# Building the state space's matrices on VectorE, in four parts between turns of an FFN's loop, instead of on GpSimd

## Chip, cores and metric

One core of one Trainium2 chip. The metric is the time of one execution of the whole program on the device, in microseconds; the median of three runs before the change is 1818.07 us (1816.41 to 1823.21).

## What is computed

A stack of four layers (256 tokens, width 1024) and one block of a second model behind it. Each layer is a mixer (attention, spatial gating, S5 state space, attention) and a gated FFN with a causal convolution of three taps. This case touches the preparation of the third layer's state space, cut here to what it computes:

```python
def s5_layer(xn, w_in, lam_re, lam_im, log_dt, b_re, b_im, c_re, c_im, d_skip, w_glu):
    ...
    mag = jnp.exp(dt * lr)
    ar = mag * jnp.cos(dt * li)
    ai = mag * jnp.sin(dt * li)
    den = lr * lr + li * li
    coef_re = ((ar - 1.0) * lr + ai * li) / den
    coef_im = (ai * lr - (ar - 1.0) * li) / den
    bbar_re = coef_re[..., None] * br32 - coef_im[..., None] * bi32
    bbar_im = coef_re[..., None] * bi32 + coef_im[..., None] * br32
    bu_re = jnp.einsum('gph,blgh->blgp', bbar_re, ug)
    ...

def conv_gated_ffn(xn, w_up, conv_w, conv_b, w_down):
    h = causal_depthwise_conv(xn @ w_up, conv_w, conv_b)
    a, g = jnp.split(h, 2, axis=-1)
    return (jax.nn.silu(g) * a) @ w_down
```

The kernel also needs the products of the decay (ar, ai) with c_re and c_im, since it works on two time steps at once.

## The kernel before

The program is written out by hand for five engines, which meet only at semaphores. SyncE streams the weights from memory in units of 128 x 2048 fp32 into a ring of three (`raw`). ScalarE rounds each unit to `whi` (`split_hi`, L385), VectorE makes the rest `wlo = raw - whi` (`split_lo`, L911), and TensorE multiplies each pair of tiles three times (L1752 to L1754: high by high, high by low, low by high). So TensorE cannot begin a unit before its L911 has ended.

An FFN has 33 units: 22 "up" and 11 "down". Two up units stand ahead of a loop of nine turns, written as a hardware loop on each engine; a turn is two up units and one down unit, and a last group of the same form follows. In a turn VectorE does, for each of the two up units: the scaling of the result out of PSUM (L1122, waits for TensorE), a split (L911, waits for ScalarE), the four convolution taps (L1136, two SBUF inputs each), a product with the gate (L1143, waits for ScalarE's SiLU at L500); then the third split and the low part of the hidden tile (L1156). The order on each engine is the order of the code, so whatever stands in front of an L911 delays it. Behind the last unit VectorE adds the result to the stream (L1200) and makes the next layer's low operand (L955). `split_hi` and `split_lo` run up to three units ahead of TensorE.

`ffn(layer, aside=None, then=None)` takes a function `aside`. With one, the loop is cut by `parts(n, cut)` into pieces of two turns, and `aside(p)` is called ahead of piece p:

```python
    return [(i, min(i + 2, n)) for i in range(0, n, 2)] if cut else [(0, n)]
...
                for p, (b, e) in enumerate(parts(n - 1, aside)):
                    if aside:
                        aside(p)
                    with dve.Fori(0, e - b) as it:
```

The nine turns make five pieces. Before the change only the fourth FFN has such a function, on ScalarE (`context_high`) and on VectorE (`context_operand`, L1087 to L1093).

GpSimd has little to do: `square_sums` (L2504) for each norm, `discretize` between the fourth and the fifth of them, during the second FFN, and later `first_inputs`, `shifted_outputs` and some products in the state space. `discretize` makes, in one chain in which almost every instruction waits for the one before it (`link`): exp(dt lr) by a polynomial on 128 x 32 (L2407 to L2418), MG as its square spread over 64 columns (L2419, L2420), a cleared area and CRE and CIM out of the DMA'd matrices SBC (L2423 to L2429), the decay ARE and AIM (L2431, L2432), the two-step decay and its 64th power (L2433 to L2443), the coefficients CFR and CFI (L2445 to L2453), and then the matrices: XB[0] from CFR, CFI and B, C2D from ARE, AIM and C (L2456 to L2469, on 64 or 128 partitions by 512). The last one sets `s5_set`, for which TensorE waits in `turn(0)` (L2276), after the first unit of the state space.

## Time and profile before

| | us |
|---|---|
| median of three runs (lowest, highest) | 1818.07 (1816.41, 1823.21) |
| the profiled execution, by the clock of the runs | 1819.32 |
| its span, first to last instruction | 1817.5 |
| TensorE (PE) busy | 1710.2, 94% |
| VectorE (DVE) busy | 1246.4, 69% |
| ScalarE (ACT) busy | 841.6, 46% |
| GpSimd (POOL) busy | 158.1, 9% |
| mean granted TensorE clock | 0.974 of full speed |

The page's chain of work that ended last is 65% TensorE and 17% VectorE. Times of instructions are counted from the start of the span. A wait in square brackets stands ahead of the instruction, with the one that ended it behind the arrow. Where an engine is busy all the time, a faster neighbour changes nothing; a change pays where it shortens a wait of the engine that sets the pace.

### The profile page before, as it was taken

Reading aid. Unit: us, or ns where it says so; the run is one execution under the profiler, and the core shown is the slowest. Engines: PE = TensorE matmul, PEld = TensorE weight load, DVE = VectorE, ACT = ScalarE, POOL = GpSimd, SP = SyncE. Lnnn points to the kernel's source line nnn. Section 1 sums busy time; section 2 is a strip of 40 time slices with the busy share of each in tenths; the row PEclk is TensorE's granted clock in tenths of the full one; section 3 lists DMA queues with packets and bytes.
Section 4 is the critical chain, followed back from the end, with each engine's and each line's share of the span. In section 5 each row is a group of like instructions: output and inputs, shape, how many; then the busy total and the mean of one; then the engine's idle time right before and its main releaser. Section 6 shows DMA issues by size and latency. Waiting matters only on the chain.

```text
span 1817.5 us, 34773 instructions
## 1 busy us (share of the span) xinstructions
PE 1710.2 (94%) x14525; PEld 1617.6 (89%) x14525; DVE 1246.4 (69%) x1592; ACT 841.6 (46%) x958; POOL 158.1 (9%) x128
## 2 busy tenths in 40 slices
PE   6999999999899998899999999999989999999997
PEld 6979999899899985699999988999988479889997
DVE  5847777786877759857777774777775575654444
ACT  5355555546445530255455445555555533143343
POOL 1002000104910062100000100100000000000000
PEclk9999999899999998999999999999989999899999
DMA  7804555535445522454555771455532221045541
GB/s 298 335 4 163 185 185 185 185 126 179 159 165 183 184 94 95 161 188 143 186 185 179 267 278 40 173 185 181 182 122 93 87 76 70 24 142 183 185 185 69
DMA packets 40050, 286.50 MB, mean 158 GB/s; under 512 B 4576, under 2 KB 4576, under 8 KB 5664
## 3 DMA queue, kind: packets, MB, share of 16 engines
q1 hardware_dynamic: 39024, 280.99, 42.9%
q10 hardware_dynamic: 944, 4.33, 0.7%
q8 instruction: 63, 1.03, 0.2%
q14 instruction: 19, 0.16, 0.0%
HBM read 284.25 MB, written 1.05 MB: 157 GB/s over the span
## 4 chain that ended last, share of the span: by engine, by line
PE 65%; DVE 17%; ACT 9%; issue 6%; POOL 1%; DMA 1%; DVEq 0%; ACTq 0%; POOLq 0%; SPq 0%
PE PS L1752 19%; PE PS L1753 19%; PE PS L1754 19%; ACT whi L385 4%; DVE wlo L911 4%; DVE AR L1136 4%; ACT AR L497 1%; DVE AR L1247 1%; DVE AR L1244 1%; ACT AR L588 1%; ACT AR L590 1%; DVE XL L955 1%; PE PS L2313 1%; PE PS L2345 1%; POOL AR L2504 1%
## 5 line engine op out<-in xcount | busy, mean ns | idle before, releaser
L1752 PE MATMUL PS<-XH,whi 128*128 128x256 f32 (+1 forms) x2696 | 787.2, 292 | 44.1 <-DVE wlo L911 33.5
L1753 PE MATMUL PS<-XL,whi 128*128 128x256 f32 (+1 forms) x2696 | 778.5, 289 | 0.0
L1754 PE MATMUL PS<-XH,wlo 128*128 128x256 f32 (+1 forms) x2696 | 778.3, 289 | 0.0
L911 DVE TENSOR_TENSOR wlo<-raw,whi 128x2048 fp32r<-128x2048 f32 x240 | 556.7, 2322 | 183.4 <-ACT whi L385 183.3
L1752 PEld LDWEIGHTS PS<-XH,whi 128*128 128x128 f32 x2696 | 521.4, 193 | 57.8 <-issue 28.3
L1753 PEld LDWEIGHTS PS<-XL,whi 128*128 128x128 f32 x2696 | 522.0, 194 | 4.5 <-issue 0.2
L1754 PEld LDWEIGHTS PS<-XH,wlo 128*128 128x128 f32 x2696 | 521.6, 193 | 4.1
L385 ACT ACTIVATE whi<-raw 128x2048 fp32r<-128x2048 f32 x240 | 456.0, 1902 | 71.4 <-PE PS L1754 46.7
L1752 PE MATMUL PS<-HH,whi 128*128 128x256 f32 x880 | 252.2, 287 | 13.0 <-DVE HL L1156 8.5
L1754 PE MATMUL PS<-HH,wlo 128*128 128x256 f32 x880 | 251.1, 285 | 0.0
L1753 PE MATMUL PS<-HL,whi 128*128 128x256 f32 x880 | 251.1, 285 | 0.0
L1752 PEld LDWEIGHTS PS<-HH,whi 128*128 128x128 f32 x880 | 170.6, 194 | 14.8 <-DVE HL L1156 9.5
L1136 DVE SCALAR_TENSOR_TENSOR AR<-AR,VEC 128x255 f32<-128x255 f32 (+1 forms) x352 | 161.5, 500 | 15.9 <-ACT AR L497 4.7
L1753 PEld LDWEIGHTS PS<-HL,whi 128*128 128x128 f32 x880 | 170.8, 194 | 0.0
L1754 PEld LDWEIGHTS PS<-HH,wlo 128*128 128x128 f32 x880 | 170.6, 194 | 0.0
L500 ACT ACTIVATE AR<-AR 128x256 f32<-128x256 f32 x88 | 36.8, 418 | 268.8 <-DVE AR L1136 268.8
L2504 POOL TENSOR_TENSOR AR<-AR 128x512 f32<-128x512 f32 x24 | 56.1, 2336 | 924.2 <-ACT AR L439 924.1
L497 ACT ACTIVATE AR<-AR,VEC 128x256 f32<-128x256 f32 x176 | 95.6, 590 | 87.0 <-DVE AR L1122 87.0
L1122 DVE TENSOR_TENSOR AR<-PS,SM 128x512 f32<-128x512 f32 x88 | 60.6, 689 | 28.1 <-PE PS L1754 25.0
L1752 PE MATMUL PS<-whi,XH 128*128 128x256 f32 x256 | 74.9, 293 | 2.1 <-DVE XL L955 2.1
L1754 PE MATMUL PS<-whi,XL 128*128 128x256 f32 x256 | 74.0, 289 | 0.0
L1753 PE MATMUL PS<-wlo,XH 128*128 128x256 f32 x256 | 73.9, 289 | 0.0
(362 smaller groups left out, 1578.7 us busy)
## 6 DMA issues: line engine op xcount, KB each, us to landing
raw<-wst SPq DMA_DIRECT2D x248, 1024.0 KB, 4.8
AR<-mst SPq DMA_DIRECT2D x17, 1024.0 KB, 5.9
XT<-x_in SPq DMA_DIRECT2D x2, 512.0 KB, 6.1
AR<-crow ACTq DMA_DIRECT2D x2, 512.0 KB, 5.8
AR<-sbc ACTq DMA_DIRECT2D x1, 1024.0 KB, 5.3
AR<-ctxin ACTq DMA_DIRECT2D x1, 1024.0 KB, 6.2
y_out<-XT SPq DMA_DIRECT2D x1, 1024.0 KB, 3.9
AR<-sgw ACTq DMA_DIRECT2D x1, 512.0 KB, 3.9
```

The lines of the kernel that those rows point to most:

```text
L385: act.activation(whi[:, r, :], raw[:, u % RING, :], ACT.Copy).then_inc(S["w_hi"], 1)
L497: a = act.activation(CA[:, j % 2, i, :], UA[:, j % 2, i, :], ACT.Identity, bias=cb, scale=w2)
L500: act.activation(SG[:, j % 2, :], CA[:, j % 2, 1, :], ACT.Silu).then_inc(S["silu_ready"], 1)
L588: act.activation(EX[:, p % 2, :], ZC[:, p % 2, :], ACT.Exp).then_inc(S["ex_ready"], 1)
L590: act.activation(LN[:, p % 2, :], EX[:, p % 2, :], ACT.Ln, bias=1.0)\
L911: dve.tensor_tensor(wlo[:, r, :], raw[:, u % RING, :], whi[:, r, :].bitcast(F32), ALU.subtract)\
L1122: dve.tensor_tensor(UA[:, j % 2], bank, RSTD.unsqueeze(1).broadcast_to([P, 2, T]), ALU.mult)\
L1136: ins = dve.scalar_tensor_tensor(y, UA[:, j % 2, i, 0:T - back], w, y, ALU.mult, ALU.add)
L1752: pe.matmul(dst, sh, mh, start=first, stop=False, **kw)
L1753: pe.matmul(dst, sh, ml, start=False, stop=False, **kw)
L1754: return pe.matmul(dst, sl, mh, start=False, stop=last, **kw)
L2504: ins = pool.tensor_tensor(SQ[:, 0:2, :], SQ[:, 0:2, :], SQ[:, 2 * mp:2 * mp + 2, :], ALU.add)
```

## The change

VectorE gets a function `matrices(p)` and makes the matrices in four parts, ahead of pieces 1 to 4 of the loop of the second FFN, which is now cut in five. GpSimd keeps the small operations on 32 columns, with those that lead to CFR and CFI brought forward, and tells VectorE with `s5_coef`; the large copies come after; at the end it waits for `s5_mats` before it sets `s5_set`.

```diff
+            def matrices(p):
+
+                if p == 0:
+                    return
+                if p == 1:
+                    dve.wait_ge(S["s5_coef"], 1)
+                    dve.wait_ge(S["s5_in"], 16)
+                b16 = lambda v: v.unsqueeze(2).broadcast_to([P, 32, 16])
+                bre, bim, cre, cim = (SBC[:, :, 16 * i:16 * i + 16] for i in range(4))
+                (c0, v0), (c1, v1), op = (((CFR, bre), (CFI, bim), ALU.subtract), ((CFR, bim), (CFI, bre), ALU.add),
+                                          ((ARE, cre), (AIM, cim), ALU.subtract), ((AIM, cre), (ARE, cim), ALU.add))[p - 1]
+                first = C2D[0] if p < 4 else C2D[1]
+                dve.tensor_tensor(first, b16(c0), v0, ALU.mult)
+                link(dve.tensor_tensor(BT, b16(c1), v1, ALU.mult))
+                if p < 3:
+                    for g in range(2):
+                        r = slice(64 * g, 64 * g + 64)
+                        ins = dve.tensor_tensor(XB[0][p - 1][r, :, 16 * g:16 * g + 16], first[r], BT[r], op)
+                    link(ins)
+                elif p == 3:
+                    link(dve.tensor_tensor(first, first, BT, op))
+                else:
+                    dve.tensor_tensor(first, first, BT, op).then_inc(S["s5_mats"], 1)
...
-            ffn(1, then=4)
+            ffn(1, aside=matrices, then=4)
...
                 pool.wait_ge(S["s5_den"], 1)
+                pool.memset(AR[:, B0:B0 + 2048], 0.0)
                 link(pool.tensor_tensor(Z5, DT, LR, ALU.mult))
...
                 link(pool.tensor_tensor(MAG2, MAG, MAG, ALU.mult))
-                link(pool.tensor_copy(MG, b64(MAG2)))
-                link(pool.memset(MG[:, :, 0:1], 0.0))
-
-                pool.wait_ge(S["s5_in"], 16)
-                link(pool.memset(AR[:, B0 + 8192:B0 + 10240], 0.0))
...
                 link(pool.tensor_tensor(ARE, MAG, COS1, ALU.mult))
                 link(pool.tensor_tensor(AIM, MAG, SIN1, ALU.mult))
+                link(pool.tensor_scalar(MAG, ARE, -1.0, None, ALU.add))
...
+                pool.tensor_tensor(CFI, T0, DEN, ALU.mult).then_inc(S["s5_coef"], 1)
+                pool.wait_ge(S["s5_coef"], 1)
                 link(pool.tensor_tensor(A2R, MAG2, TC[:, :, 1], ALU.mult))
...
-                link(pool.memset(AR[:, B0:B0 + 2048], 0.0))
-                for xb, (c0, v0), (c1, v1), op in ((XB[0][0], (CFR, bre), (CFI, bim), ALU.subtract),
-                                                   (XB[0][1], (CFR, bim), (CFI, bre), ALU.add)):
-                    for r, h in halves:
-                        ins = pool.tensor_tensor(xb[r, :, h], b16(c0)[r], v0[r], ALU.mult)
-                    link(ins)
-                    link(pool.tensor_tensor(BT, b16(c1), v1, ALU.mult))
-                    for r, h in halves:
-                        ins = pool.tensor_tensor(xb[r, :, h], xb[r, :, h], BT[r], op)
-                    link(ins)
-                for o, c0, c1, op in ((C2D[0], ARE, AIM, ALU.subtract), (C2D[1], AIM, ARE, ALU.add)):
...
+                link(pool.tensor_copy(MG, b64(MAG2)))
+
+                pool.wait_ge(S["s5_in"], 16)
+                link(pool.memset(AR[:, B0 + 8192:B0 + 10240], 0.0))
...
+                pool.wait_ge(S["s5_mats"], 1)
+                pool.memset(MG[:, :, 0:1], 0.0).then_inc(S["s5_set"], 1)
                 pool.wait_ge(S["s5_set"], 1)
```

**VectorE, the end of a turn of the second FFN's loop.** Before, the loop's branch goes back eight times and the rows behind it are the group after the loop:

```order
L911 TENSOR_TENSOR wlo<-raw,whi 128x2048 [waits w_hi]
L1155 REGISTER_ALU
L1156 TENSOR_TENSOR HL<-AR,HH 128x512 [waits hh_ready]
L1172 REGISTER_ALU
L1172 COMPARE_AND_BRANCH
L1122 TENSOR_TENSOR AR<-PS,SM 128x512 [waits w_used]
```

With the change, the branch goes back once in a piece of two turns, and part 1 stands behind it (L1296 and L1297 the two products, L1301 their difference into XB[0][0]):

```order
L1156 TENSOR_TENSOR HL<-AR,HH 128x512 [waits hh_ready]
L1172 REGISTER_ALU
L1172 COMPARE_AND_BRANCH
L1296 TENSOR_TENSOR AR<-AR 128x512 [waits s5_in,s5_coef]
L1297 TENSOR_TENSOR AR<-AR 128x512
L1301 TENSOR_TENSOR AR<-AR 64x32x16 [waits link]
L1301 TENSOR_TENSOR AR<-AR 64x32x16
L1172 UNCONDITIONAL_BRANCH [waits link]
L1172 ISA
L1122 TENSOR_TENSOR AR<-PS,SM 128x512 [waits w_used]
```

Four operations and the entry of a new loop have come between L1156 and the next L1122. Part 2 has the same form; parts 3 and 4 have one operation on 128x512 in place of the two L1301.

**GpSimd, the end of `discretize`.** Before, the last products and the next square sum:

```order
L2467 TENSOR_TENSOR AR<-SM,AR 128x512 [waits s5_step]
L2468 TENSOR_TENSOR AR<-SM,AR 128x512
L2469 TENSOR_TENSOR AR<-AR 128x512 [waits s5_step]
L2504 TENSOR_TENSOR AR<-AR 128x512 [waits square,s5_set]
```

With the change, the copies (MG, then CRE and CIM) and the wait for VectorE (line numbers are those of the changed kernel; L2512 is the square sum):

```order
L2469 COPY AR<-AR 128x2048 [waits s5_step]
L2472 MEMSET AR 128x2048 [waits s5_in,s5_step]
L2477 COPY AR<-AR 64x32x16 [waits s5_step]
L2478 TENSOR_SCALAR AR<-AR 64x32x16
L2477 COPY AR<-AR 64x32x16 [waits s5_step]
L2478 TENSOR_SCALAR AR<-AR 64x32x16
L2480 MEMSET AR 128x32 [waits s5_mats,s5_step]
L2512 TENSOR_TENSOR AR<-AR 128x512 [waits square,s5_set]
```

The large copies have moved from the middle of the chain to its end, and the sixteen products are gone.

## Rows read from the trace of the kernel before

**Rows 1.** The page, busy time of each engine and its share of the span
```profile
PE 1710.2 (94%) x14525; PEld 1617.6 (89%) x14525; DVE 1246.4 (69%) x1592; ACT 841.6 (46%) x958; POOL 158.1 (9%) x128
```
**Rows 2.** Windows, first and second FFN: length, busy PE, PEld, DVE, ACT, POOL
```profile
149.40:343.40 194.00, 190.75 (x1579) 189.46 (x1578) 145.94 (x183) 101.68 (x116) 3.20 (x1) 1.00 0.50 178
433.60:637.15 203.55, 192.77 (x1579) 191.06 (x1578) 157.61 (x184) 101.82 (x116) 64.44 (x76) 0.99 0.49 175
```
**Rows 3.** Waits of TensorE, second FFN, then first: total, times, longest
```profile
PE PS L1752 <- DVE wlo L911: 8.6, 5, 3.4
...
PE PS L1752 <- DVE wlo L911: 1.1, 3, 0.4
```
**Rows 4.** Timeline of TensorE at the two long waits: start, duration, wait
```profile
494.81 0.39 PE L1752 MATMUL PS<-XH,whi 128*128 128x256 f32 x1 [3.37 <-DVE wlo L911]
...
509.41 0.39 PE L1752 MATMUL PS<-XH,whi 128*128 128x256 f32 x1 [2.83 <-DVE wlo L911]
```
**Rows 5.** A window behind them; behind POOL stand granted clock, DMA share, GB/s
```profile
510.00:515.00 5.00, 5.00 (x32) 5.00 (x31) 3.00 (x5) 3.80 (x4) 0.00 (x0) 0.66 0.53 210
```
**Rows 6.** VectorE's groups, 481 to 506.5 us, then 529.9 to 564.5 us
```profile
L1136 DVE SCALAR_TENSOR_TENSOR AR<-AR,VEC 128x255 f32<-128x255 f32 (+1 forms) x8 | 10.2, 1308 | 0.3
L911 DVE TENSOR_TENSOR wlo<-raw,whi 128x2048 fp32r<-128x2048 f32 x3 | 8.5, 2831 | 1.9 <-ACT whi L385 1.9
...
L1122 DVE TENSOR_TENSOR AR<-PS,SM 128x512 f32<-128x512 f32 x2 | 1.4, 677 | 0.0
...
L911 DVE TENSOR_TENSOR wlo<-raw,whi 128x2048 fp32r<-128x2048 f32 x6 | 13.7, 2288 | 3.8 <-ACT whi L385 3.8
L1136 DVE SCALAR_TENSOR_TENSOR AR<-AR,VEC 128x255 f32<-128x255 f32 (+1 forms) x16 | 7.0, 479 | 0.6
```
**Rows 7.** Timeline of GpSimd: a small operation, the first products, the last one
```profile
465.22 2.35 POOL L2431 TENSOR_TENSOR SM<-AR,SM 128x32 f32<-128x32 f32 x1
...
480.88 4.13 POOL L2460 TENSOR_TENSOR AR<-AR 64x512 f32<-64x512 f32 x2
...
505.78 1.35 POOL L2469 TENSOR_TENSOR AR<-AR 128x512 f32<-128x512 f32 x1
```
**Rows 8.** Timeline of VectorE, undisturbed loop of the second FFN
```profile
551.53 0.69 DVE L1122 TENSOR_TENSOR AR<-PS,SM 128x512 f32<-128x512 f32 x1 [0.99 <-PE PS L1754]
```
**Rows 9.** Timelines of VectorE, then TensorE, at the fourth FFN's second piece
```profile
1198.33 0.88 DVE L1089 SCALAR_TENSOR_TENSOR AR<-AR,MODG 128x256 f32<-128x256 f32 x2
...
1201.59 2.29 DVE L911 TENSOR_TENSOR wlo<-raw,whi 128x2048 fp32r<-128x2048 f32 x1 [0.99 <-ACT whi L385]
...
1205.18 0.88 DVE L1136 SCALAR_TENSOR_TENSOR AR<-AR,VEC 128x254 f32<-128x254 f32 x2 [0.50 <-DVE AR L1136]
...
1217.08 0.39 PE L1752 MATMUL PS<-XH,whi 128*128 128x256 f32 x1 [0.38 <-DVE wlo L911]
```
**Rows 10.** Timeline of VectorE while GpSimd makes MG, CRE and CIM
```profile
455.66 1.90 DVE L1156 TENSOR_TENSOR HL<-AR,HH 128x512 fp32r<-128x512 f32 x1 [0.70 <-ACT HH L513]
...
460.28 2.60 DVE L1136 SCALAR_TENSOR_TENSOR AR<-AR,VEC 128x255 f32<-128x255 f32 x4
```
**Rows 11.** Timeline of VectorE in the spatial gating ahead of the second FFN
```profile
364.79 0.19 DVE L1272 TENSOR_TENSOR SM<-SM 128x32 f32<-128x32 f32 x1
365.01 2.29 DVE L1273 TENSOR_TENSOR AR<-SM,CST 128x2048 f32<-128x2048 f32 x1
...
400.00 1.29 DVE L1322 TENSOR_TENSOR AR<-AR 128x512 f32<-128x512 f32 x2
```
**Rows 12.** Timeline of TensorE, the first work that waits for `s5_set`
```profile
651.97 3.29 PE L2276 MATMUL PS<-CST,AR 128*128 128x128 f32 x28
```
**Rows 13.** Windows, sum of 455.1 to 457.05 and 459.1 to 465.2, GpSimd only
```profile
sum 8.05, POOL 7.74; mean POOL 3.87
```
**Rows 14.** Queues (packets, MB, share of 16 engines); DMA issues (KB, us to landing)
```profile
q8 instruction: 63, 1.03, 0.2%
...
VEC<-vec SPq DMA_DIRECT2D x1, 36.0 KB, 1.7
```

More of the change, by code:

```diff
@@ L289, in program @@
                  "gelu5", "silu_c", "scp_nil", "mod_rows", "mod_sum", "mod_vec", "ctx_in", "mod_gain",
-                 "c_in", "c_row", "x5_last", "ctx_rms", "ctx_inv", "ctx_diag", "ctx_row", "gains2", "second", "second_rms", "row_diag", "row_twice", "ml_in0", "ml_in1", "ml_used",
+                 "c_in", "c_row", "s5_coef", "s5_mats", "x5_last", "ctx_rms", "ctx_inv", "ctx_diag", "ctx_row", "gains2", "second", "second_rms", "row_diag", "row_twice", "ml_in0", "ml_in1", "ml_used",
                  "normed", "wide_taken", "csq", "csum", "crms", "crinv", "cnormed", "kv_part", "q_out", "rot",
@@ L2418, in discretize @@
                 link(pool.tensor_tensor(MAG2, MAG, MAG, ALU.mult))
-                link(pool.tensor_copy(MG, b64(MAG2)))
-                link(pool.memset(MG[:, :, 0:1], 0.0))
-                pool.wait_ge(S["s5_in"], 16)
-                link(pool.memset(AR[:, B0 + 8192:B0 + 10240], 0.0))
-                bre, bim, cre, cim = (SBC[:, :, 16 * i:16 * i + 16] for i in range(4))
-                for g in range(2):
-                    r = slice(64 * g, 64 * g + 64)
-                    h = slice(16 * g, 16 * g + 16)
-                    pool.tensor_copy(CRE[r, :, h], cre[r])
-                    link(pool.tensor_scalar(CIM[r, :, h], cim[r], -1.0, None, ALU.mult))
                 pool.wait_ge(S["s5_table"], 4)
@@ L2432, in discretize @@
                 link(pool.tensor_tensor(AIM, MAG, SIN1, ALU.mult))
+                link(pool.tensor_scalar(MAG, ARE, -1.0, None, ALU.add))
+                link(pool.tensor_tensor(T0, MAG, LR, ALU.mult))
+                link(pool.tensor_tensor(T1, AIM, LI, ALU.mult))
+                link(pool.tensor_tensor(T0, T0, T1, ALU.add))
+                link(pool.tensor_tensor(CFR, T0, DEN, ALU.mult))
+                link(pool.tensor_tensor(T0, MAG, LI, ALU.mult))
+                link(pool.tensor_tensor(T1, AIM, LR, ALU.mult))
+                link(pool.tensor_tensor(T0, T1, T0, ALU.subtract))
+                pool.tensor_tensor(CFI, T0, DEN, ALU.mult).then_inc(S["s5_coef"], 1)
+                pool.wait_ge(S["s5_coef"], 1)
                 link(pool.tensor_tensor(A2R, MAG2, TC[:, :, 1], ALU.mult))
@@ L2444, in discretize @@
                 complex_product(AER, AEI, (A2R, A2I), (TC[:, :, 63], TS[:, :, 63]))
-                link(pool.tensor_scalar(MAG, ARE, -1.0, None, ALU.add))
-                link(pool.tensor_tensor(T0, MAG, LR, ALU.mult))
-                link(pool.tensor_tensor(T1, AIM, LI, ALU.mult))
-                link(pool.tensor_tensor(T0, T0, T1, ALU.add))
-                link(pool.tensor_tensor(CFR, T0, DEN, ALU.mult))
-                link(pool.tensor_tensor(T0, MAG, LI, ALU.mult))
-                link(pool.tensor_tensor(T1, AIM, LR, ALU.mult))
@@ L2452, in discretize @@
-                link(pool.tensor_tensor(T0, T1, T0, ALU.subtract))
-                link(pool.tensor_tensor(CFI, T0, DEN, ALU.mult))
-                halves = [(slice(64 * g, 64 * g + 64), slice(16 * g, 16 * g + 16)) for g in range(2)]
-                link(pool.memset(AR[:, B0:B0 + 2048], 0.0))
-                for xb, (c0, v0), (c1, v1), op in ((XB[0][0], (CFR, bre), (CFI, bim), ALU.subtract),
-                                                   (XB[0][1], (CFR, bim), (CFI, bre), ALU.add)):
-                    for r, h in halves:
-                        ins = pool.tensor_tensor(xb[r, :, h], b16(c0)[r], v0[r], ALU.mult)
-                    link(ins)
-                    link(pool.tensor_tensor(BT, b16(c1), v1, ALU.mult))
-                    for r, h in halves:
-                        ins = pool.tensor_tensor(xb[r, :, h], xb[r, :, h], BT[r], op)
-                    link(ins)
@@ L2466, in discretize @@
-                for o, c0, c1, op in ((C2D[0], ARE, AIM, ALU.subtract), (C2D[1], AIM, ARE, ALU.add)):
-                    pool.tensor_tensor(o, b16(c0), cre, ALU.mult)
-                    link(pool.tensor_tensor(BT, b16(c1), cim, ALU.mult))
-                    ins = pool.tensor_tensor(o, o, BT, op)
-                    if op == ALU.subtract:
-                        link(ins)
-                ins.then_inc(S["s5_set"], 1)
+                link(pool.tensor_copy(MG, b64(MAG2)))
+                pool.wait_ge(S["s5_in"], 16)
@@ new lines, in discretize @@
+                link(pool.memset(AR[:, B0 + 8192:B0 + 10240], 0.0))
+                bre, bim, cre, cim = (SBC[:, :, 16 * i:16 * i + 16] for i in range(4))
+                for g in range(2):
+                    r = slice(64 * g, 64 * g + 64)
+                    h = slice(16 * g, 16 * g + 16)
+                    pool.tensor_copy(CRE[r, :, h], cre[r])
+                    link(pool.tensor_scalar(CIM[r, :, h], cim[r], -1.0, None, ALU.mult))
+                pool.wait_ge(S["s5_mats"], 1)
+                pool.memset(MG[:, :, 0:1], 0.0).then_inc(S["s5_set"], 1)
```

## The prediction

> **What bounds the kernel now.** I first read the busy times: TensorE is busy for 94% of the span, and GpSimd, whose work is being changed, for 9% [rows 1]. So GpSimd's own time is worth nothing as such; the change can pay only where GpSimd or VectorE makes TensorE wait. The place to look is the second FFN, and a good yardstick lies beside it: the four FFNs run the same loop. The windows put each from VectorE's last residual addition before it to its first one behind the loop [rows 2]. The first FFN, with one GpSimd instruction in the window, takes 194.0 us. The second, with 64.4 us of GpSimd, takes 203.55 us. The excess is 9.5 us: that is all that can be had here.
>
> The waits say what it is made of. In the second FFN TensorE waits 8.6 us for `wlo`, in five waits, the longest 3.4 us; in the first 1.1 us in three [rows 3]. That is 7.5 us of the 9.5. The two long waits (3.37 and 2.83 us) end at 494.81 and 509.41 [rows 4]. Behind the second, the granted clock averages 0.66 over 5 us [rows 5], between its levels of 1.2 and 2.4 GHz, which costs 5 x 0.34 = 1.7 us. The sum is 9.2, and the rest is the restart of each wait.
>
> Why `wlo` is late is seen on VectorE. From 481 to 506.5 us, its convolution taps (L1136) take 1308 ns each and the split of a weight unit (L911) 2831 ns; two undisturbed turns give 479 and 2288 ns [rows 6]. The extra is 8 x 0.83 = 6.6 us and 3 x 0.54 = 1.6 us, together 8.2 us. L1122, which reads PSUM and one SBUF tile, is as fast as ever (677 ns against 0.69 us [rows 6, 8]). That stretch is exactly GpSimd's large multiplications: it begins them at 480.88 and ends at about 507.1 [rows 7]. So the two engines slow each other where both read SBUF, and the lateness reaches TensorE.
>
> **How much lateness TensorE stands.** A turn of the loop is three weight units of TensorE. In an undisturbed one VectorE waits 1.00 us for TensorE [rows 8]: that is what it can make up per turn. The fourth FFN shows the rest, since its VectorE loop is already cut in the same five pieces with work between. Its second piece of work is four operations in the 1.6 us from 1198.33; then the split starts 0.99 us late by ScalarE's own extra work, and 0.36 us go as gaps in a loop entered anew (0.50 us shown before the taps). Together 2.95, less 1.00, is a lag of 1.95 us, and TensorE restarts 0.54 us late (0.38 shown, and 0.16 of slow first matmul) [rows 9]. So a lag of about 1.4 us is free. What is over becomes a stall, and after a stall 1.4 us of lag is left, of which the next turn takes back 1.0.
>
> **The change, part by part.**
> *Taken from GpSimd:* 16 instructions, 480.9 to 507.1 us. With them go both long waits, 2 x about 3.25 us with their restarts, and the slow clock behind them, 1.7 us: 8.2 us. The memset that stood just ahead of them moves to the chain's start, and I cost it at nothing: VectorE was not slowed beside it. What then stays of the excess is 203.55 - 194.0 - 8.2 = 1.3 us.
> *Moved on GpSimd:* the small operations to CFI now stand ahead of the copies. The polynomial ended where the copy of MG began, at 455.1 us [rows 13]; 1.8 us of memset and 11 operations of 0.3 to 2.4 us (some 13.7 us passed from 465.22 until the multiplications' memset for 19 of them) put `s5_coef` at 463 to 468 us. Part 1 on VectorE comes after two turns, at about 491 (the long wait of 3.37 us that ends at 494.81 began then). Cover 23 us, so this wait costs nothing. The copy of MG and the four instructions on CRE and CIM, which read SBUF, move from 455 to 465 us to about 470 to 482. Beside them VectorE lost 1.2 us on L1156 (1.90 against the 0.69 of its shape) and 0.7 us on L1136 (2.60 against 4 x 0.48) [rows 6, 10, 11], and TensorE's three short waits, 8.6 - 3.37 - 2.83 = 2.4 us, were 1.3 us longer than the three of the first FFN. I expect the same 1.9 us of lag one turn later. VectorE enters that turn with 0.4 us left over: 0.4 + 1.9 is 0.9 over 1.4. Stall 0.9 us.
> *Added to VectorE:* parts 1 and 2 are two operations on 128x512 and two on 64 partitions of 512; parts 3 and 4 are three on 128x512. Two back to back on SBUF take 1.29 us, so 0.60 each and 0.69 for the last; a row with a broadcast operand (L1273) takes 2.29 us for 2048 columns, no more than L911; a link adds 0.04 us (364.79 + 0.19 to 365.01) [rows 11]. No row has the 64-partition shape on VectorE: between 0.3 us (as half the work) and 0.7 us, I take 0.60, because all time here goes with columns. So 2.64, 2.64, 2.04 and 1.92 us, 9.2 in all.
> Part 1 meets a VectorE that has just stalled TensorE: 1.4 - 1.0 left + 2.64 + 0.36 of loop entry = 3.4, stall 2.0 us. Part 2, two turns later: 0.4 + 2.64 - 1.0 = 2.05, stall 0.6. Part 3: 0.4 + 2.04 - 1.0 = 1.45, none. Part 4: 1.3, none, and 0.3 us of lag at the loop's tail, which I count in full.
> *The new end:* GpSimd waits for `s5_mats`, set after eight of the nine turns, some 35 us before the FFN ends at 637.15 [rows 2], and then clears one column of MG. Behind that wait stand only its next square sums, which need the FFN's result, and TensorE wants `s5_set` after the first unit of the state space, from 651.97 us [rows 12]. Cover 40 us: nothing. ScalarE's and TensorE's instructions and all DMAs stay in place.
> *Sum:* 194.0 + 0.9 + 2.0 + 0.6 + 0.3 = 197.8 us against 203.55, a gain of 5.7 us. The profiled execution took 1819.3 us (its span of 1817.5 and 1.8 around it), so it would take 1813.6. That execution lies 1.25 above the median of the runs, 1818.07; from the median I predict **1812.4 us**.
>
> **A rule that speaks against it.** The rows show a two-sided collision: a 32-column operation of GpSimd that takes 0.3 us elsewhere took 2.35 at 465.22, when a 2.29 us split ran [rows 7, 10]. The Trainium skill, "SBUF — State Buffer", "Who interferes with whom", says that a VectorE instruction with two SBUF inputs contends with a GpSimd one that reads SBUF, and that the later of the two is held until the other is done. By that page's rule VectorE could lose the whole duration of the five reading instructions that remain; the lag would be several times that of the row. The sum goes by the row's 1.9; a full block is the second rival, priced there from rows.
>
> **The rivals.**
> 1. *All of it hides.* The copies fall where VectorE is not behind and the parts stay under 1.4 us of lag: the second FFN becomes as long as the first, gain 8 to 9.5 us, 1808.6 to 1810. For it: part 1 without the stall before it costs only 0.6. Against: 9.2 us of new work against some 1.0 us a turn to make up. Chance 0.14, half of it past the bound of 0.5%.
> 2. *The remaining GpSimd reads hold VectorE in full.* The five took 7.74 us [rows 13]: that much lag instead of 1.9, 5.8 us more of stall, and the clock may fall again (1.7). That gives 1812.4 + 5.8 = 1818.2, or 1820. Against: before, the same instructions cost 1.9. For it: they now fall in a turn that is already late. Chance 0.12.
> 3. *The cut loop stalls at its entries, and it is slower.* VectorE now has five loops in place of one, and each must be fetched. The page has 63 instruction packets with 0.2% of 16 engines' span, 0.92 us each, and the smallest DMA lands after 1.7 us [rows 14]: at most 2.6 us per entry if VectorE waits for each. Four entries: 10.4 us, 208.2 us for the FFN, 1822.8 in all. It turns the gain into a loss from 5.7 / 4 = 1.4 us per entry; to pass 0.5% the branches back must wait as well (eight places, 1833). The Trainium skill, "Runtime: NRT & Kernel Launch", "Instruction fetch mechanics", says that a taken branch out of the prefetched window forces a fetch by DMA. Against: the fourth FFN's second entry shows 0.50 us of gap, and its VectorE runs the same five loops. Chance 0.04, most of it past the bound.
> 4. *GpSimd was not the cause* and nothing moves (within 1 us). Against: L1136 is slow exactly while GpSimd multiplies. Chance 0.02.
>
> **The numbers.** The forecast with its own spread (the stall of part 1 0.6 or 2.3, a fall of the clock of 1.7 or none, gain 3 to 8 us) has 0.68. The range reaches from all 9.5 us gained, 1808.6, to none, 1818.0, which leaves rival 3 and half of rival 2 outside. A difference of 0.5% is 9.1 us, about what a measurement can tell from no change here. Faster by that needs practically the whole excess: 0.08, half of rival 1 and a little for scatter between runs (1816.4 to 1823.2). Slower by that: 0.03. Within: 0.89.
>
> **What would show it.** The second FFN at 197.8 us in the window from VectorE's last residual addition to its first after the loop. No wait over 3 us in it; waits for `wlo` of some 3.5 us in all. GpSimd's chain ends at about 480 us, and L1136 stays near 480 ns from there. One stall of about 2 us behind part 1 and one of 0.6 behind part 2, none behind parts 3 and 4. Gaps of at most 0.5 us at the loop entries. It is wrong if TensorE waits over 1 us behind parts 3 or 4 (the parts are longer than 2.6 us), if VectorE waits for `s5_coef`, if L1296 to L1301 take over 0.8 us each, or if the state space starts later.

## The result and the profile after

The changed kernel takes **1808.38 us** (median of 5 runs, 1807.82 to 1811.29) against 1818.07 (1816.41 to 1823.21): the ratio is 0.9946, with an interval of 0.9929 to 0.9962. The profiled execution took 1808.38 us itself, with a span of 1806.6. The forecast was 1812.4 with a range from 1808.6 to 1818.0: the gain is 9.7 us where 5.7 were expected, and the time lies 0.2 us below the range.

The page after has 27.3 us less work on GpSimd and 16 instructions fewer (compare [rows 1]); VectorE did not get busier in spite of its 14 new instructions:

```profile
PE 1701.0 (94%) x14511; PEld 1609.8 (89%) x14525; DVE 1246.5 (69%) x1606; ACT 841.6 (47%) x958; POOL 130.8 (7%) x112
...
L1136 DVE SCALAR_TENSOR_TENSOR AR<-AR,VEC 128x255 f32<-128x255 f32 (+1 forms) x352 | 154.8, 481 | 15.2 <-ACT AR L497 4.7
```

The 9.4 us of matrices (2.71, 2.71, 2.01 and 2.01 us for the four parts) are paid for by what VectorE no longer loses to the collision: its taps were 6.6 us slower while GpSimd multiplied [rows 6]. The same windows as in [rows 2], first and second FFN:

```profile
149.00:343.00 194.00, 190.67 (x1571) 189.30 (x1571) 144.91 (x183) 101.06 (x116) 3.97 (x2) 1.00 0.50 179
433.51:630.26 196.75, 191.94 (x1569) 189.78 (x1569) 156.97 (x198) 101.80 (x116) 37.12 (x60) 0.99 0.51 181
```

The second FFN fell from 203.55 to 196.75 us, by 6.8; 1.05 us less than the 197.8 forecast. TensorE's waits there, and in the first FFN (to set beside [rows 3]):

```profile
PE PS L1776 <- DVE wlo L911: 2.6, 7, 0.4
...
PE PS L1776 <- DVE wlo L911: 1.1, 3, 0.4
```

Seven waits of at most 0.4 us instead of five with two of about 3. Three belong to the loop's beginning, as in the first FFN. The other four, in TensorE's timeline:

```profile
496.19 0.39 PE L1776 MATMUL PS<-HH,whi 128*128 128x256 f32 x1 [0.33 <-DVE wlo L911]
...
502.59 0.39 PE L1776 MATMUL PS<-XH,whi 128*128 128x256 f32 x1 [0.38 <-DVE wlo L911]
...
508.98 0.39 PE L1776 MATMUL PS<-XH,whi 128*128 128x256 f32 x1 [0.39 <-DVE wlo L911]
...
544.29 0.39 PE L1776 MATMUL PS<-XH,whi 128*128 128x256 f32 x1 [0.38 <-DVE wlo L911]
```

Three stand behind part 1 and one behind part 2, none behind parts 3 and 4. With its slow first matmul (0.16 us) each is worth 0.49 to 0.54 us. Below, such a sum is called a stall with its restart. VectorE at part 1 (start, duration; the gap of 0.22 us is the entry of the next loop), and its groups from 481 to 506.5 us, where L1136 had 1308 ns and L911 2831 [rows 6]:

```profile
490.32 0.68 DVE L1296 TENSOR_TENSOR AR<-AR 128x512 f32<-128x512 f32 x1
490.92 0.69 DVE L1297 TENSOR_TENSOR AR<-AR 128x512 f32<-128x512 f32 x1
491.64 1.39 DVE L1301 TENSOR_TENSOR AR<-AR 64x512 f32<-64x512 f32 x2
493.25 0.69 DVE L1122 TENSOR_TENSOR AR<-PS,SM 128x512 f32<-128x512 f32 x1 [0.22 <-DVE AR L1301]
...
L911 DVE TENSOR_TENSOR wlo<-raw,whi 128x2048 fp32r<-128x2048 f32 x4 | 9.2, 2290 | 2.9 <-ACT whi L385 2.9
L1136 DVE SCALAR_TENSOR_TENSOR AR<-AR,VEC 128x255 f32<-128x255 f32 (+1 forms) x12 | 5.3, 479 | 0.4
```

GpSimd's copies, which now stand last, and VectorE beside them:

```profile
468.09 1.89 POOL L2469 COPY AR<-AR 128x2048 f32<-128x2048 f32 x1
...
471.91 1.05 POOL L2477 COPY AR<-AR 64x512 f32<-64x512 f32 x1
472.93 1.93 POOL L2478 TENSOR_SCALAR AR<-AR 64x512 f32<-64x512 f32 x1
...
597.68 0.15 POOL L2480 MEMSET AR<- 128x32 f32 x1 [119.28 <-DVE AR L1306]
```
```profile
468.39 1.86 DVE L1143 TENSOR_TENSOR AR<-AR 128x256 f32<-128x256 f32 x1 [0.48 <-ACT AR L500]
...
472.41 1.10 DVE L1156 TENSOR_TENSOR HL<-AR,HH 128x512 fp32r<-128x512 f32 x1
...
476.23 2.60 DVE L1136 SCALAR_TENSOR_TENSOR AR<-AR,VEC 128x255 f32<-128x255 f32 x4
```

L1143 takes 1.86 us where it takes 0.43 elsewhere, L1156 1.10 for 0.69, the four taps 2.60 for 1.89: 2.6 us lost, and TensorE does not stop for it at once.

**Outside the second FFN.** The span fell by 10.9 us, of which the second FFN has 6.8. The fourth FFN, where nothing was changed, is 0.5 us shorter (198.89 to 198.38), the part behind it 3.3 (478.92 to 475.63), and the stretches between second and fourth 0.3 together. This the forecast did not have, and the experiments had to say whether it belongs to the change.

### The profile page after: what moved, and what is told of

It reads as the page before. It is cut to its first block, busy times and chain, and to the rows that moved or that the text cites. A ratio compares the mean times of both kernels' runs of the same rounds, so it can differ in the third digit from the quotient of the medians.

```text
span 1806.6 us, 34747 instructions
## 1 busy us (share of the span) xinstructions
PE 1701.0 (94%) x14511; PEld 1609.8 (89%) x14525; DVE 1246.5 (69%) x1606; ACT 841.6 (47%) x958; POOL 130.8 (7%) x112
## 3 DMA queue, kind: packets, MB, share of 16 engines
HBM read 284.25 MB, written 1.05 MB: 158 GB/s over the span
## 4 chain that ended last, share of the span: by engine, by line
PE 63%; DVE 17%; ACT 10%; issue 6%; POOL 2%; DMA 1%; DVEq 0%; ACTq 0%; POOLq 0%; SPq 0%
PE PS L1776 18%; PE PS L1778 18%; PE PS L1777 18%; ACT whi L385 5%; DVE wlo L911 4%; DVE AR L1136 4%; ACT AR L497 2%; POOL AR L2512 1%; DVE AR L1247 1%; DVE AR L1244 1%; ACT AR L588 1%; ACT AR L590 1%; DVE XL L955 1%; PE PS L2369 1%; PE PS L2151 1%
## 5 line engine op out<-in xcount | busy, mean ns | idle before, releaser
L911 DVE TENSOR_TENSOR wlo<-raw,whi 128x2048 fp32r<-128x2048 f32 x240 | 555.1, 2315 | 184.0 <-ACT whi L385 183.9
L1136 DVE SCALAR_TENSOR_TENSOR AR<-AR,VEC 128x255 f32<-128x255 f32 (+1 forms) x352 | 154.8, 481 | 15.2 <-ACT AR L497 4.7
L2512 POOL TENSOR_TENSOR AR<-AR 128x512 f32<-128x512 f32 x24 | 56.1, 2337 | 827.9 <-ACT AR L439 827.8
L1122 DVE TENSOR_TENSOR AR<-PS,SM 128x512 f32<-128x512 f32 x88 | 60.6, 689 | 21.3 <-PE PS L1778 18.4
```

Source lines behind the costliest of these rows:

```text
L911: dve.tensor_tensor(wlo[:, r, :], raw[:, u % RING, :], whi[:, r, :].bitcast(F32), ALU.subtract)\
L1122: dve.tensor_tensor(UA[:, j % 2], bank, RSTD.unsqueeze(1).broadcast_to([P, 2, T]), ALU.mult)\
L1136: ins = dve.scalar_tensor_tensor(y, UA[:, j % 2, i, 0:T - back], w, y, ALU.mult, ALU.add)
L2512: ins = pool.tensor_tensor(SQ[:, 0:2, :], SQ[:, 0:2, :], SQ[:, 2 * mp:2 * mp + 2, :], ALU.add)
```

## The experiments

Each kernel was timed beside runs of the kernel before on the same chip; these had medians of 1817.24, 1817.05, 1817.0 and 1816.62 us (e1 to e4, e5 to e8, e9 to e11, e12). Second FFN means the window from VectorE's last residual addition ahead of it to its first behind the loop, from each profile.

| kernel | median us (lowest to highest) | ratio and interval | second FFN | fourth FFN | behind it |
|---|---|---|---|---|---|
| before | | | 203.6 | 198.9 | 478.9 |
| changed | 1808.38 (1807.8 to 1811.3) | 0.9946 [0.9929, 0.9962] | 196.8 | 198.4 | 475.6 |
| e1 | 1809.15 (1806.5 to 1811.3) | 0.9949 [0.9933, 0.9966] | 196.8 | 198.4 | 475.6 |
| e2 | 1808.28 (1806.2 to 1811.8) | 0.9945 [0.9929, 0.9961] | 195.4 | 198.9 | 477.0 |
| e3 | 1814.29 (1812.0 to 1819.4) | 0.9984 [0.9972, 0.9996] | 202.7 | 198.4 | 475.7 |
| e4 | 1816.99 (1815.5 to 1821.8) | 0.9995 [0.9983, 1.0007] | 202.0 | 198.9 | 479.0 |
| e5 | 1806.50 (1805.5 to 1807.6) | 0.9942 [0.9927, 0.9958] | 195.6 | 198.4 | 475.7 |
| e6 | 1816.24 (1813.4 to 1819.5) | 0.9996 [0.9986, 1.0005] | 203.1 | 198.4 | 477.1 |
| e7 | 1814.52 (1811.8 to 1819.2) | 0.9986 [0.9975, 0.9997] | 202.2 | 198.4 | 475.7 |
| e8 | 1817.58 (1814.4 to 1824.5) | 1.0004 [0.9993, 1.0015] | 203.3 | 198.5 | 477.1 |
| e9 | 1816.02 (1811.7 to 1817.3) | 0.9990 [0.9981, 0.9999] | 194.6 | 198.5 | 477.3 |
| e10 | 1816.18 (1812.3 to 1820.5) | 0.9995 [0.9985, 1.0006] | 195.3 | 198.5 | 477.1 |
| e11 | 1810.89 (1808.3 to 1814.3) | 0.9961 [0.9947, 0.9974] | 196.8 | 198.5 | 477.1 |
| e12 | 1809.70 (1807.5 to 1810.9) | 0.9956 [0.9941, 0.9971] | 195.2 | 198.4 | 477.2 |

### e1: the changed kernel again

> The changed kernel once more, for a second profile. Theory 1 (lateness): the second FFN takes 196.75 us again, within 0.3, with the same four waits behind parts 1 and 2. What the whole gained beyond that stretch (10.9 us of span in the first pair of profiles against 6.8 in the FFN) is stretches at half clock elsewhere, which fall differently from run to run: the whole then gains 6 to 10 us in the median, and the half-clock stretches outside the FFN stand at other places than in the first profile. Rival (the rest of the gain is fixed): the same 4 us are missing outside the FFN at the same places, between 650 and 760 us and behind 1340 us.

The second FFN comes back as 196.81 us with the same seven waits, so this number belongs to the kernel. The whole is 8.1 us under the kernel before beside it, not 9.7.

### e2: the products out

The kernel before, with its sixteen large operations left out (the state space's input matrices stay at zero and C2D is only cleared):

```diff
-                for xb, (c0, v0), (c1, v1), op in ((XB[0][0], (CFR, bre), (CFI, bim), ALU.subtract),
...
+                ins = pool.memset(AR[:, B0 + 7168:B0 + 8192], 0.0)
                 ins.then_inc(S["s5_set"], 1)
```

> The kernel before with GpSimd's sixteen products of the state space's matrices left out (a memset of C2D stands for them, XB stays zero), nothing added to VectorE; the first part of the computation that is missing is the matrices. Theory 1: the collision with the products is the whole cost beyond the early 1.3 us, so the second FFN takes 194.0 + 1.3 = 195.3 us, with no wait over 1.5 us, and the whole takes 8.2 us less than before, 1809.9. Rival (the cost lies in the chain as a whole, small operations too): it stays above 198 us. Rival (clock): the whole gains 3 us more than the FFN, 1807, as with the change.

Both long waits are gone with the products, in a loop that is not cut: 203.6 becomes 195.35 us. So the products are the cause, and with nothing given to VectorE in return they are worth 8.2 us of the 9.5, just what the forecast worked out from two waits and a stretch at the lower clock. What stays are the three waits at the loop's beginning, of 1.12, 1.24 and 0.55 us with their restarts, beside the copies at 455 us; their longest is

```profile
PE PS L1752 <- DVE wlo L911: 2.4, 3, 1.1
```

### e3: only the loop cut

The kernel before, with VectorE's loop in the second FFN cut in five and nothing between the pieces:

```diff
-            ffn(1, then=4)
+            ffn(1, aside=lambda p: None, then=4)
```

> The kernel before with VectorE's loop of the second FFN cut in five pieces and nothing between them. Theory 1: 0 to 0.4 us more lag at each entry, which shows only where VectorE is late already: the FFN takes 203.5 to 204.2 us and the whole is unchanged within 1 us. Rival (a loop entered anew must be fetched): 2.6 us at each of four entries, of which at least 4 us reach TensorE, 207 us or more.

The entries cost nothing that can be seen: the second FFN takes 202.66 us, 0.9 less than uncut, since the second long stall (2.99 us with its restart) turned into one of 1.61 and one of 0.55. The windows between the two stalls, in the kernel before and in e3, show why (the third figure from the end is the granted clock):

```profile
494.80:509.40 14.60, 11.78 (x96) 11.57 (x96) 13.49 (x11) 4.30 (x6) 11.95 (x8) 1.00 0.40 144
...
494.70:509.30 14.60, 13.14 (x96) 12.94 (x96) 13.48 (x11) 4.30 (x6) 11.99 (x8) 0.89 0.40 144
```

VectorE, beside GpSimd, takes the same 14.6 us in both. In e3 the clock falls in this stretch, so TensorE needs more of it for the same work and waits less at its end; before, it falls behind the second stall, where its 1.7 us are lost. Behind this stretch the kernel before loses those 1.7 us and e3 the 0.55 of the short stall: 1.15 us apart by this estimate, 0.9 as measured. In e4 (clock 0.81 between the stalls) and e8, whose second FFN is not cut, it falls there as well. So the 0.9 us go with the place of the fall and not with the cut.

### e4: only GpSimd's new order

The changed kernel with the sixteen products back on GpSimd, behind the copies, and the loop whole:

```diff
-            ffn(1, aside=matrices, then=4)
+            ffn(1, then=4)
...
-                pool.wait_ge(S["s5_mats"], 1)
-                pool.memset(MG[:, :, 0:1], 0.0).then_inc(S["s5_set"], 1)
+                link(pool.memset(MG[:, :, 0:1], 0.0))
...
+                ins.then_inc(S["s5_set"], 1)
```

> The changed kernel's order of GpSimd's chain, but the sixteen products stay on GpSimd, at its end; VectorE's loop is whole. Theory 1: the products collide with VectorE wherever they stand, so the FFN takes 202 to 204 us again and the whole is within 1.5 us of before. Rival (the order did it): the early waits shrink and the FFN falls below 200 us.

The three waits at the loop's beginning shrink to 0.52, 0.63 and 0.55 us, since the copies no longer stand there. The products still cost most of what they did: a long stall of 3.98 us with the lower clock behind it, and two short ones (waits of 0.19 and 0.38 us), stand in place of the two. VectorE's taps of 481 to 512 us are slow again, 1032 ns over a longer stretch than that of [rows 6] with its 1308:

```profile
L1136 DVE SCALAR_TENSOR_TENSOR AR<-AR,VEC 128x255 f32<-128x255 f32 (+1 forms) x12 | 11.9, 1032 | 0.4
```

The order alone is worth 1.6 us in the second FFN and nothing measurable in the whole.

### e5: the copies out

The changed kernel with the copies of MG, CRE and CIM left out (MG is cleared instead, CRE and CIM stay at zero):

```diff
-                link(pool.tensor_copy(MG, b64(MAG2)))
+                link(pool.memset(AR[:, B0 + 4096:B0 + 6144], 0.0))
...
-                    pool.tensor_copy(CRE[r, :, h], cre[r])
-                    link(pool.tensor_scalar(CIM[r, :, h], cim[r], -1.0, None, ALU.mult))
```

> The changed kernel without GpSimd's five remaining instructions that read SBUF at length (the copy of MG, and the four on CRE and CIM; memsets stand in, so MG, CRE and CIM are zero). Theory 1: beside them VectorE lost 2.5 us in the changed kernel, which TensorE did not see at once but which left VectorE at the edge of the free 1.4 us when part 1 began; without them part 1 costs one wait of 0.5 us in place of three of 0.5, and the second FFN takes 195.6 us. Rival (the lateness was made good before part 1): 196.8 us and the same three waits.

The second FFN takes 195.61 us, and of the three waits behind part 1 one remains (0.55 us with its restart), as behind part 2. So two of the three, 1.0 us (1.1 in the FFN's time), are the lag of the copies, carried over two turns until part 1 comes on top.

```profile
PE PS L1776 <- DVE wlo L911: 1.9, 5, 0.4
```

### e6: all four parts in one place

```diff
-            ffn(1, aside=matrices, then=4)
+            ffn(1, aside=lambda p: [matrices(q) for q in (1, 2, 3, 4)] if p == 1 else None, then=4)
```

> The changed kernel with all four parts in one lump ahead of piece 1, the loop still cut. Theory 1: lateness beyond 1.4 us is a stall whatever idle time VectorE has later: 0.4 + 9.3 + 0.2 - 1.0 - 1.4 = 7.5 us of waits in place of 2.1, the second FFN at 202 us. Rival (only the sum of VectorE's work in the FFN counts): 196.8 us as with four parts.

The same four parts on VectorE, 9.5 us from 490.54 to 500.01 us, in one lump:

```profile
502.95 0.58 PE L1776 MATMUL PS<-HH,whi 128*128 128x256 f32 x1 [6.86 <-DVE wlo L911]
```

```profile
500.00:507.00 7.00, 4.05 (x19) 4.05 (x20) 5.60 (x10) 3.35 (x5) 0.15 (x1) 0.51 0.39 140
507.00:514.00 7.00, 7.00 (x60) 7.00 (x60) 4.99 (x7) 3.82 (x6) 0.00 (x0) 1.00 0.48 159
```

One stall of 7.02 us with its restart, behind which the granted clock (the tenth figure of a window, behind POOL) is 0.51, the lower level, up to 507 us. The second FFN takes 203.05 us: all that the move had gained is lost again. That the work is spread over turns is what makes it cheap.

### e7: longer parts

Each part repeats its two products, 1.5 us more per part:

```diff
                 dve.tensor_tensor(first, b16(c0), v0, ALU.mult)
+                link(dve.tensor_tensor(BT, b16(c1), v1, ALU.mult))
+                link(dve.tensor_tensor(first, b16(c0), v0, ALU.mult))
                 link(dve.tensor_tensor(BT, b16(c1), v1, ALU.mult))
```

> The changed kernel with the two products of each part done twice, 1.3 us more in each of the four. Theory 1: parts 3 and 4, which cost nothing, were just inside the free lag, so every part now costs about its 1.3 us: waits of 2.9, 1.8, 1.3 and 1.2 us, the second FFN at 201.5 to 202 us. Rival (parts 3 and 4 had room left): 199.4 us, with waits behind parts 1 and 2 alone.

```profile
PE PS L1778 <- DVE wlo L911: 6.4, 13, 1.8
```

The second FFN takes 202.2 us. The stalls, each with its restart: 1.93, 0.53, 0.54 behind part 1; 0.83, 0.53, 0.54 behind part 2 (1.90); 0.55 and 0.53 behind part 3 (1.08); 0.38 and 0.43 behind part 4. A part of 4.17 us (part 2) with 0.22 of entry therefore costs 1.9, and one of 2.71 costs 0.54: what a turn stands is 2.4 to 2.5 us, the forecast's 1.4 of free lag and 1.0 made up. Part 3, 3.5 + 0.2 - 2.4 = 1.3, is near its 1.08; part 4, 3.5 - 2.4 = 1.1 (it has no gap at its entry), is above its 0.81. So the model holds to about 0.3 us.

### e8: the cut in the first FFN

> The kernel before with VectorE's loop cut in the first FFN in place of the second, nothing between the pieces. The uncut kernels had 198.9 us in the fourth FFN and 477 to 479 us behind it, the cut ones 198.4 and 475.6, though nothing was changed there. Theory A (place of VectorE's later instructions in its stream): the same 198.4 and 475.6 us, and the whole 2 to 3 us faster than before. Theory B (an effect of the second FFN's own course): 198.9 and 477 to 479 us, the whole unchanged. Either way the first FFN takes 194.0 to 194.4 us and the second 203.5.

The edit is that of e3, in `ffn(0, then=2)`. The first FFN stays at 194.0 us. The fourth takes 198.45, as in every kernel with an additional cut, but what follows it takes 477.1, and the whole is not faster (1.0004, interval 0.9993 to 1.0015). Theory A is right for the 0.5 us of the fourth FFN and wrong for the rest.

### e9: halves, and the output side in the state space

The input side's two matrices are halved (products in one place, sums in the next); the output side's two move to the start of the state space, where VectorE waits for TensorE (ScalarE and GpSimd then wait there for `s5_mats` as well):

```diff
+                matrix((p - 1) // 2, BT)[(p - 1) % 2]()
...
             def state_space(i):
                 scales()
+                for m in (2, 3):
+                    for f in matrix(m, BT):
+                        f()
                 dve.wait_ge(S["s5_set"], 1)
```

> The same work in other places: the two matrices of the input side stay between the turns of the second FFN's loop, but each is halved (two products in one place, the two half sums in the next), so that no place has more than 1.4 us; the two of the output side (4 us) go to the start of the state space, where VectorE waits 4.5 us for TensorE. Lag theory: a piece of 1.4 us stays under what TensorE stands behind parts 2 to 4, so of the four waits behind the parts at most the first remains, which holds the copies' lag; second FFN 195.2 to 195.8 us (changed kernel 196.8); nothing is lost in the state space; whole 1 to 1.5 us under the changed kernel. Rival (VectorE's time at the state space's start is not free, because GpSimd's first inputs run there on SBUF and the two slow each other): the second FFN gains its 1 us, and 1 to 4 us come back between the second FFN's end and the third's; whole the same as the changed kernel or up to 3 us over it.

Both theories came true, and more strongly than expected. The second FFN takes 194.57 us, 0.6 below the lag theory's range: behind the first half stands one wait of 0.16 us, behind the others none, so of the excess of 9.5 only 0.5 is left, and the copies' lag costs next to nothing if only 1.3 us of work come on top. And the rival's collision is back in the state space. GpSimd makes its first inputs there:

```profile
647.50 2.40 POOL L2505 TENSOR_TENSOR AR<-SM,AR 128x1024 f32<-128x1024 f32 x1
649.97 2.72 POOL L2506 TENSOR_TENSOR AR<-AR 128x1024 f32<-128x1024 f32 x1
```
```profile
647.42 0.69 DVE L1294 TENSOR_TENSOR AR<-SM,AR 128x512 f32<-128x512 f32 x1
648.03 2.41 DVE L1295 TENSOR_TENSOR AR<-SM,AR 128x512 f32<-128x512 f32 x1
650.47 2.76 DVE L1303 TENSOR_TENSOR AR<-AR 128x512 f32<-128x512 f32 x1
653.27 0.69 DVE L1294 TENSOR_TENSOR AR<-SM,AR 128x512 f32<-128x512 f32 x1
```
```profile
656.25 0.58 PE L1790 MATMUL PS<-XH,whi 128*128 128x256 f32 x1 [3.79 <-DVE AR L984]
```

Operations of 0.69 us take 2.41 and 2.76: each begins 0.5 us behind one of GpSimd's and ends 0.5 us behind its end. TensorE waits 3.79 us for the scaled result behind them, and its next matmuls take 0.41 us each in place of 0.28, since the granted clock is at its lower level there (0.50 from 656.2 to 661.2). From the second FFN's end to VectorE's memset behind the scaled results, in e9 and in e11 (the changed kernel):

```profile
625.60:676.21 50.61, 41.05 (x423) 39.82 (x422) 28.38 (x33) 16.44 (x22) 26.86 (x14) 0.90 0.23 84
...
629.39:673.51 44.12, 38.35 (x422) 37.19 (x421) 24.11 (x26) 16.42 (x22) 26.02 (x14) 0.96 0.26 96
```

That is 6.5 us lost: the wait, and a longer time at the lower clock. The changed kernel's other two profiles have 42.6 and 44.8 us there. With the 2.2 us gained in the FFN, 4.3 us remain; the medians of e9 and e11 lie 5.1 apart, which is more than the rival had expected.

### e10: the input side whole, one place later

> As e9, but the two input-side matrices whole, in the second and third places (two turns later than in the changed kernel), with nothing in the first and fourth. Lag theory (the three waits behind part 1 of the changed kernel come from the copies' lag two turns before, and a part of 2.6 us on its own makes one wait of 0.54, as part 2 showed): one wait of 0.54 us behind each of the two parts, second FFN 195.6 to 195.8 us. Rival (the first part costs three waits wherever it stands): 196.3 to 196.7 us.

As e9, with part 1 in the second place and part 2 in the third. Behind each stands one wait (0.51 and 0.45 us with restart), and the second FFN takes 195.26 us. Two turns more are enough to pay the copies' lag: the extra waits in the changed kernel are a matter of the place. From the second FFN's end to the memset it takes 50.0 us, with the collision in the same place as in e9; so the whole, 1816.18, is no better than e9's.

### e11: the changed kernel beside e9 and e10

> The changed kernel once more, beside e9 and e10 on the same chip: second FFN 196.8 us, 1807 to 1810 us in all.

The second FFN is 196.80 us again, but behind the fourth stand 477.1 us, not 475.6, and the whole is 1810.89. So this difference, which up to e5 seemed to go with the cut loop, occurs **within one kernel**. A window of the changed kernel's first profile, and one of e11, over the same work:

```profile
1336.00:1350.00 14.00, 10.94 (x43) 9.06 (x43) 11.10 (x32) 5.80 (x11) 0.00 (x0) 0.63 0.22 77
```
```profile
1339.00:1355.00 16.00, 12.94 (x44) 10.74 (x45) 11.88 (x37) 5.87 (x12) 0.00 (x0) 0.59 0.19 66
```

The tenth figure is the granted clock: 14 x 0.37 / 0.5 = 10.4 us at the lower level in the first, 16 x 0.41 / 0.5 = 13.1 us in the second. The 2.7 us between them cost about 1.4, nearly all of the 1.5 us by which e11 is longer behind the fourth FFN. The other 1.8 us, between e11 and the kernel before, are a clock's too. The kernel before and e11, over the same 40 us of work 218 us behind the fourth FFN:

```profile
1556.61:1596.61 40.00, 36.13 (x268) 32.98 (x268) 24.91 (x33) 9.88 (x11) 0.00 (x0) 0.87 0.16 54
...
1551.41:1591.41 40.00, 36.50 (x283) 33.04 (x284) 25.25 (x34) 10.85 (x13) 0.00 (x0) 0.91 0.18 57
```

40 x 0.13 / 0.5 = 10.4 us at the lower level against 7.2, and the difference costs 1.6. So nearly all of the 3.3 us behind the fourth FFN go with the clock. That the clock falls there less because of the change is not shown.

That the time of the whole goes with the clock is seen in the runs' lists: over 81 executions of the kernel before beside these experiments (one more, of 2366 us at a clock of 0.649, is left out), the time falls by 0.90 us for each 0.001 of mean granted clock, with a correlation of -0.89 (1814.2 us at 0.979, 1823.2 at 0.970). Brought to a clock of 0.977 by this slope, their mean is 1816.9; the changed kernel's three groups of runs give 1810.9, 1810.4 and 1811.8, which is 6.0, 6.6 and 5.1 us less. That is an estimate, as the change may itself move the clock, but it is near the second FFN's 6.8.

### e12: half a part before every turn

The likeliest version to beat the change: all four matrices in the second FFN, halved, one half before each turn from the third on, eight places (`fine` is true in the second FFN alone):

```diff
-                for p, (b, e) in enumerate(parts(n - 1, aside)):
+                pieces = [(0, 2)] + [(k, k + 1) for k in range(2, n - 1)] if fine else parts(n - 1, aside)
+                for p, (b, e) in enumerate(pieces):
...
+                if fine:
+                    aside(8)
```

> All four matrices stay in the second FFN, halved as in e9 (products in one place, sums in the next), one half before each turn from the third on, eight places in all (seven single turns of the loop instead of three pairs and one). Lag theory: each turn brings 1.3 us of work (2 x 0.6 and a link; the last halves of the output side 0.7) and 0.1 to 0.2 us of entry, and takes back 1.0; the copies' lag is there as before, so over the input side's four turns the lag grows by 1.2 to 2.0 us, then falls: stalls of 1 to 1.6 us in all instead of 2.1, second FFN 195.8 to 196.4 us (changed kernel 196.8, e9 194.6). The whole 0.5 to 1 us under the changed kernel, which its scatter hides. Rival (seven loops of one turn cost VectorE 0.5 us each at their entry): 197 to 199 us.

```profile
PE PS L1791 <- DVE HL L1156: 2.1, 1, 2.1
PE PS L1791 <- DVE wlo L911: 1.2, 3, 0.4
```

No wait stands behind any half: only the three at the loop's beginning are left, and the second FFN takes 195.17 us, 0.6 less than expected and 1.6 less than with the change. It is still 1.1 us longer than the first FFN. Five turns take TensorE 17.38 to 17.48 us where the first FFN's take 17.28, 0.7 in all, and no wait shows it. The entry of a loop of one turn costs 0.12 us:

```profile
490.92 0.68 DVE L1299 TENSOR_TENSOR AR<-AR 128x512 f32<-128x512 f32 x1
491.72 0.69 DVE L1122 TENSOR_TENSOR AR<-PS,SM 128x512 f32<-128x512 f32 x1
```

The one place too near the end shows in the wait for HL, 2.1 us for 1.8. In the whole, 1809.70 us beside a before of 1816.62, it cannot be told from the changed kernel, whose three medians are 1808.4, 1809.2 and 1810.9.

## Why the prediction was right and wrong

**Right: the cause and its worth.** Taking the products from GpSimd was put at 8.2 us; e2 shows 203.56 - 195.35 = 8.2. Rival 4 is out. That it agrees to a tenth is in part luck: it holds for a course in which the clock falls behind the second stall, and by e3 a fall between the stalls makes the loss 0.9 us smaller.

**Right: the cost of the parts.** Worked out were 2.64, 2.64, 2.04 and 1.92 us, measured 2.71, 2.71, 2.01 and 2.01; the 64-partition operations take 0.68 to 0.69 us each, as long as those on 128 partitions, not half. The stall behind part 2 was put at 0.6 us and is 0.54; behind parts 3 and 4 none was expected and none came. The model (1.4 us of lag free, 1.0 made up per turn) was drawn from one stall of the fourth FFN, and e7 bears it out at another size, to about 0.3 us.

**Right: the new end.** GpSimd waits 119 us for `s5_mats` and nobody waits for it. `s5_coef` stood at 463 us, 27 us ahead of its use.

**Mis-sized: "Stall 0.9 us" for the copies and "stall 2.0 us" behind part 1.** Together 2.9 us, measured 1.57. The copies did slow VectorE, by 2.6 us and more than the 1.9 estimated, but did not stop TensorE. The step that failed is in these two sums. "0.4 + 1.9 is 0.9 over 1.4" and "1.4 - 1.0 left + 2.64 + 0.36 of loop entry = 3.4" leave out the 1.0 us that VectorE makes up in the turn itself, which the sums for parts 2 to 4 do take off (and those leave out the entry). With it, the forecast's own figures give 0.4 + 1.9 - 1.0 = 1.3 for the copies, under 1.4 and so no stall, as measured, and 3.4 - 1.0 - 1.4 = 1.0 for part 1. And for part 1 they count on 0.4 us of lag where more was left. What the runs show: a part of this size with no lag before it has 2.71 + 0.22 - 2.4 = 0.53 (0.55 in e5), and the copies leave 1.0 us of lag for part 1 (1.57 - 0.55). That 1.0 is read off the same runs; a check on it is e9, where a half comes in the same place: 1.29 + 0.22 + 1.0 - 2.4 = 0.1, and 0.3 us with its restart were measured.

**Mis-sized: the loop's entry.** 0.36 us were taken from the fourth FFN; in the second it is 0.22 (none at part 4), in e12 0.12. And the 0.50 us that the forecast read as a gap of the entry stands 5 us behind it, among the taps. Rival 3 is out: e3, with four entries and nothing else, is not slower. By the Trainium skill's page "Runtime: NRT & Kernel Launch", "Instruction fetch mechanics", a taken branch out of the prefetched window has to wait for a fetch; none of these gaps comes near the 1.7 us of the smallest DMA [rows 14]. The fourth FFN's own 0.50 us before the taps [rows 9] is there in the three kernels without an additional cut (before, e2, e4) and in none of the others, whose fourth FFN takes 198.4 to 198.5 us for 198.9. So that gap goes with the cut, wherever it is made; that it depends on where the instructions lie, and is a fetch, is only argued.

The sum of what was measured: 194.03 + 1.57 + 0.54 = 196.14; the 0.6 us left to 196.75, put down to the tail and the entries, was not measured by itself, where 0.3 had been put for the tail. The three waits at the loop's beginning went back to those of the first FFN by the order alone, as e4 shows, where the forecast moved their 1.3 us to the copies' new place as its 0.9. Together the second FFN came out 1.05 us under the forecast, within the forecast's own spread.

**Wrong, and what put the time outside the range: "that is all that can be had here", as an end for the whole.** For the second FFN it holds (e9 took 9.0 of the 9.5). But the low end of the range, 1808.6, set the whole excess against one median, as if nothing else moved. The time of the whole moves with the granted clock by several us from execution to execution: the same changed kernel gave a gain of 9.7, 8.1 and 6.1 us. Of the first, 6.8 are the second FFN and 0.5 the fourth; the other 2.4 are not shown to be the change's: e11 is the same kernel with 1.5 us less of the gain behind the fourth FFN, where the clock makes the difference, and the other two gains are smaller by 1.6 and 3.6. That the first measurement fell just outside the range is thus in part chance; by the second FFN alone it would have been 1811.3. Rival 1 had put the time at 1808.6 to 1810 with a second FFN as long as the first; that FFN took 196.75 us, so the whole came near rival 1's time for another reason. The range lacked a term for this scatter between medians, some 2 us either way, though the kernel before already had 1816.4 to 1823.2 in its own runs.

**Rival 2, the full block.** For the five remaining reads it did not come: no stall of 5.8 us. By the rule of the Trainium skill's page "SBUF — State Buffer", "Who interferes with whom", the later of two such instructions is held until the other is done. In e9 single operations look just so (0.69 us becomes 2.41 and 2.76 beside GpSimd's 2.40 and 2.72), while the four taps at 476.23, beside a GpSimd operation of 1.57 us (L2478), lost only 0.7. The rule fits those single pairs; what it costs a stage depends on how the two fall, and the rows, not the rule, came nearer here: 1.9 us of lag expected, 2.6 measured, 7.7 for a full hold.

**Left open:** what moves the stretches at the lower clock, why five turns of e12 are 0.1 to 0.2 us longer with no wait to show for it, and what makes the gap among the fourth FFN's taps.

## What to carry to other kernels

An engine with spare time per turn can take foreign work for nothing if no place gets more than a turn stands (here 2.4 us), and if it does not fall on the lag of something else. The same work on VectorE made TensorE stall for 7.0 us in one lump, 2.1 in four parts and not at all in eight; the FFN was 9.0, 2.7 and 1.1 us longer than the undisturbed one. Moved work must not meet the engine it was moved away from: e9 gained 2.2 us in the FFN and lost 6.5 in the state space to the same collision and the lower clock behind it. What a fall of the clock costs depends on where it comes: next to nothing where VectorE sets the pace (the 14.6 us of e3), and by estimate half its length where TensorE does. When a local gain is known from the trace, give the range of the whole the scatter between medians as well, and check a surplus by running the same kernel again before explaining it.

## What was not expected of the hardware

The mean granted clock alone tells the time of an execution of the kernel before to about 1 us (81 executions, 0.90 us per 0.001), and the stretches at half speed lie in other places from one execution of a kernel to the next. GpSimd's small operations suffer as well: one of 32 columns took 2.29 us at 457.49, beside a split of 2.29 us, where its neighbours take 0.25 to 0.55.
